# Two transformer blocks on one Trainium2 core: sliding attention one head at a time beside the rotary products, with values stationary; retention normalised head by head; probabilities scaled on GpSimd

## The reference

```python
q_a, k_a, v_a, q_r, k_r, v_r, g_r = jnp.split(rms_norm(x, g) @ w_in, splits, axis=-1)
# sliding attention: 8 heads of 64, two key/value heads, blocks of 128 queries
# see their own 128 keys (causal) and the 128 before (those within the window)
probs = softmax(concat([scores / 8, sink]))[..., :-1];  attn = probs @ v_a
# retention: 4 heads of 128, q and k turned by position, decay in place of softmax
o = (rot(q_r) @ rot(k_r).T * decay) @ v_r           # causal, all 512 tokens
o = (o - mean(o)) * rsqrt(var(o) + eps)             # for each token and head
ret = silu(g_r) * o
x = x + rms_norm(concat([attn, ret]) @ w_out, post)
```

## Time and profile before

| | |
|---|---|
| median of three runs | 2179.32 us (2174.88 to 2185.81) |
| the profiled execution | 2190.08 us, its span 2188.3 us |
| TensorE busy (PE) | 2093.4 us, 96% of the span |
| VectorE, ScalarE, GpSimd busy | 1043.9 us (48%), 822.4 us (38%), 279.7 us (13%) |
| mean granted TensorE clock | 0.973 |
| the chain that ended last, by engine | PE 80%, DVE 6%, ACT 4%, POOL 4%, issue 2% |

### The profile page before, as it was taken

The page is one execution under the profiler, slowest core; times in us unless marked ns, Lnnn a source line. Parts: engine busy times, 40 slices in busy tenths (PEclk is TensorE's granted clock), DMA queues, the critical chain, the costliest instruction groups (busy, mean ns, idle before and its releaser), DMA issues.

```text
span 2188.3 us, 25825 instructions
## 1 busy us (share of the span) xinstructions
PE 2093.4 (96%) x10292; PEld 1741.5 (80%) x10292; DVE 1043.9 (48%) x1627; ACT 822.4 (38%) x1518; POOL 279.7 (13%) x271
## 2 busy tenths in 40 slices
PE   7999999999999999999999899899999999999998
PEld 6878888888878888887887679677777888888886
DVE  5436465555335222333654666665655544222333
ACT  5225253333334222233324653355555323222232
POOL 1000100000000000000002422166664000000000
PEclk9997799999999999999999899999999999999999
DMA  5330133333322323332442034211114423333331
GB/s 193 111 92 1 49 107 96 97 96 96 97 87 97 93 92 95 97 96 77 139 141 68 1 123 142 73 58 44 44 44 147 135 75 106 96 96 97 97 96 68
DMA packets 58983, 200.14 MB, mean 91 GB/s; under 512 B 8080, under 2 KB 8112, under 8 KB 58480
## 3 DMA queue, kind: packets, MB, share of 16 engines
q1 hardware_dynamic: 53936, 178.29, 26.2%
q0 software_dynamic: 4928, 20.21, 2.6%
HBM read 181.16 MB, written 8.39 MB: 87 GB/s over the span
## 4 chain that ended last, share of the span: by engine, by line
PE 80%; DVE 6%; ACT 4%; POOL 4%; issue 2%; DVEq 1%; DMA 1%; POOLq 1%; SPq 0%; ACTq 0%
PE ps L655 25%; PE ps L654 25%; PE ps L653 25%; POOL PU L609 4%; DMA raw<-in_w_all 1%; PE ps L1067 1%; ACT Pb L1354 1%; DVE XN L1690 1%; DVE HTl L1699 1%; PE ps L983 1%; DVEq L2185 1%; DVE AUl L2190 1%; PE ps L828 1%; POOLq L598 1%; PE ps L898 1%
## 5 line engine op out<-in xcount | busy, mean ns | idle before, releaser
L1650 DVE TENSOR_TENSOR Wl<-raw,Wh 128x1024 fp32r<-128x1024 f32 x307 | 378.0, 1234 | 784.2 <-ACT Wh L1188 783.2
L653 PE MATMUL ps<-HTh,Wh 128*128 128x512 f32 (+1 forms) x1696 | 642.6, 379 | 15.9 <-DVE HTl L1699 9.7
L655 PE MATMUL ps<-HTh,Wl 128*128 128x512 f32 (+1 forms) x1696 | 647.5, 382 | 0.0
L654 PE MATMUL ps<-HTl,Wh 128*128 128x512 f32 (+1 forms) x1696 | 646.3, 381 | 0.0
L1188 ACT CAST Wh<-raw 128x1024 fp32r<-128x1024 f32 x307 | 321.2, 1050 | 841.0 <-DMA raw<-in_w_all 841.0
L653 PEld LDWEIGHTS ps<-HTh,Wh 128*128 128x128 f32 x1696 | 326.7, 193 | 81.1 <-issue 15.2
L654 PEld LDWEIGHTS ps<-HTl,Wh 128*128 128x128 f32 x1696 | 320.7, 189 | 60.9
L655 PEld LDWEIGHTS ps<-HTh,Wl 128*128 128x128 f32 x1696 | 320.5, 189 | 58.1
L653 PE MATMUL ps<-Wh,Yh 128*128 128x512 f32 x528 | 208.1, 394 | 4.3 <-DVE Yl L1826 4.3
L655 PE MATMUL ps<-Wh,Yl 128*128 128x512 f32 x528 | 206.5, 391 | 0.0
L654 PE MATMUL ps<-Wl,Yh 128*128 128x512 f32 x528 | 205.0, 388 | 0.0
(11 more groups left out here) (273 smaller groups left out, 2524.5 us busy)
## 6 DMA issues: line engine op xcount, KB each, us to landing
raw<-in_w_all SPq DMA_DIRECT2D x307, 512.0 KB, 3.5
swp_d<-qkd SPq DMA_DIRECT2D x64, 64.0 KB, 2.8
g_dram<-gst SPq DMA_DIRECT2D x16, 256.0 KB, 4.0
ring<-g_dram POOLq DMA_DIRECT2D x16, 256.0 KB, 3.6
gpre<-in_g_pre POOLq DMA_DIRECT2D x5, 512.0 KB, 5.0
X<-in_x SPq DMA_DIRECT2D x4, 512.0 KB, 5.1
swp_r<-qkr SPq DMA_DIRECT2D x16, 128.0 KB, 3.8
cw1k<-in_cw POOLq DMA_DIRECT2D x1, 2048.0 KB, 8.3
```

Of the source, the lines that this page charges most:

```text
L653: tensor.matmul(dst, a_hi, b_hi, start=start, stop=False)
L654: tensor.matmul(dst, a_hi, b_lo, start=False, stop=False)
L655: return tensor.matmul(dst, a_lo, b_hi, start=False, stop=stop)
L1650: vector.tensor_tensor(Wl[:, s, :], raw[:, s, :], Wh[:, s, :], ALU.subtract).then_inc(w_lo, 1)
```

## The change

1. **Sliding attention becomes eight units, one for each head**, in the form of the sparse stage: scores of the four query tiles in banks 0 and 1 (128 + 256 and 256 + 256 columns), four maxima with the sink, four exponentials, factors, scaling on GpSimd, seven transposes into banks 2 and 3, high and low parts, and values as stationary operand (`vhla`, high and low part side by side) into bank 4 or 5. The result is already transposed (`CATT`), so it needs no transposes later. The mask is one bf16 product of up to 256 columns (`band`).
2. **These units stand between the chunks of `rope_r`**, which uses banks 6 and 7 only. Beside the last two units stand the products of `vg`'s first four chunks for token tile 3, in the same two banks. The wait for masks and preparations comes after the first rotary chunk.
3. **Retention is normalised head by head**: statistics straight from PSUM, one square root for each head, normalising into `CAT` on VectorE, gate product on GpSimd, four transposes on TensorE into bank 6 or 7.
4. **`out1` starts with attention's four chunks**, first for token tiles 0 and 1, then, after the transposes of heads 2 and 3, for tiles 2 and 3. `cat` is gone.
5. GpSimd's loads of `cos`, `sin` and `gpost` come before the gate products, that of `gpre` after them.
6. **`cmp_vals` moves from behind the fifth to behind the seventh product of `rope_q`**, and ScalarE's share (zeros filled with values, `vcz`) with it.
7. Places in SBUF change (`slots` starts at another offset, `cst` moves). The helpers of `da` lose the case distinction; their instructions stay.

```diff
-    ("rope_r", 8, [2, 2, 2, 2, 0, 0, 0, 0], [0] * 8),
+    ("rope_r", 8, [0, 0, 0, 0, 0, 0, 4, 4], [0] * 8),
+    ("local", 0, [0] * 8, [8, 8, 8, 8, 4, 4, 0, 0]),
...
-        slots = (nc.sbuf_base + 127) // 128 * 128
+        slots = (nc.sbuf_base + 383) // 512 * 512 + 128
...
+        LOCAL = [(0, 0, 0, 0), (0, 128, 128, 1), (1, 0, 384, 2), (1, 256, 640, 3)]
...
+                def local_weigh(h):
+                    pl.wait_ge(l_gate, h + 1)
+                    for b, o, p, i in LOCAL:
+                        w = P if i == 0 else 2 * P
+                        x = PL[:, h % 2, p:p + w]
+                        last = pool.tensor_scalar(x, x, lsum[:, h % 2, i:i + 1], None, ALU.mult)
+                    last.then_inc(l_prob, 1)
...
-                pl.wait_ge(gn_rs, 1)
-                pool.tensor_tensor(ret_out, ret_out, by_tile(mv[:, :, 0]), ALU.subtract)
-                pool.drain()
-                pool.tensor_tensor(ret_out, ret_out, by_tile(grs[:]), ALU.mult)
-                pool.drain()
...
-                pool.tensor_tensor(CAT[:, :, 512:], CAT[:, :, 512:], sg[:], ALU.mult).then_inc(cat_ret, 1)
+                def gated(h):
+                    one = slice(h * P, (h + 1) * P)
+                    pl.wait_ge(free[4 + h % 2], FREED["ret"][4 + h % 2] + h // 2 + 1)
+                    pool.tensor_tensor(CAT[:, :, one], CAT[:, :, one], sg[:, :, one], ALU.mult).then_inc(cat_ret, 1)
...
+                def local_scores(h):
+                    kv = h // 4
+                    for b, o, p, i in LOCAL:
+                        if i % 2 == 0:
+                            bank_free("local", b, h)
+                        w = P if i == 0 else 2 * P
+                        k = slice(0, P) if i == 0 else slice((i - 1) * P, (i + 1) * P)
+                        q = qa[h // 4][:, h % 4, i * P:(i + 1) * P]
+                        dst = ps[b][:, o:o + w]
+                        tensor.matmul(dst, q, kah[:, kv, k], start=True, stop=False)
+                        tensor.matmul(dst, q, kal[:, kv, k], start=False, stop=False)
+                        last = tensor.matmul(dst, identb[:], band[:, 2 * P - w:], start=False, stop=True)
...
+                def local_values(h):
...
+                        tensor.matmul(dst, v, ALh[:, a], start=kb == 0, stop=False)
+                        last = tensor.matmul(dst, v, ALl[:, a], start=False, stop=kb == 3)
...
+                rope_r(0)
+                pe.wait_ge(in_c2, 16 * 9)
+                pe.wait_ge(boot, 2)
...
+                local_scores(0)
+                local_scores(1)
+                rope_r(1)
+                for h in range(8):
+                    local_turn(h)
+                    if h < 6:
+                        local_scores(h + 2)
+                        rope_r(h + 2)
+                    else:
+                        vg(2 * (h - 6), (3,), False)
+                        vg(2 * (h - 6) + 1, (3,), False)
+                    local_values(h)
             if on("vg"):
-                gemm_t("vg")
+                for c in range(4):
+                    vg(c, (0, 1, 2), True)
+                for c in range(4, 8):
+                    vg(c, range(TT), True)
...
+                ret_scores(0)
+                ret_scores(1)
                 for b in range(8):
                     pe.wait_ge(free[b], FREED[ret][b])
...
+                ret_values(0)
+                ret_scores(2)
+                ret_values(1)
+                ret_scores(3)
+                ret_turn(0)
+                ret_values(2)
+                ret_turn(1)
+                ret_values(3)
+                pe.wait_ge(ct_lo, 4)
+                for c in range(4):
+                    chunk_t("out1", c, *ht_lhs(c), c == 0, False, tiles=(0, 1), last_part=False)
+                ret_turn(2)
+                ret_turn(3)
+                for c in range(4):
+                    chunk_t("out1", c, *ht_lhs(c), c == 0, False, tiles=(2, 3))
...
-                cmp_vals()
                 rope_q(5)
                 rope_q(6)
+                cmp_vals()
                 cmp_turn(0)
...
+                rope_out(0)
+                local_exps(0)
+                rope_out(1)
+                local_exps(1)
+                for h in range(8):
+                    local_high(h)
+                    if h:
+                        local_low_rows(h - 1)
+                    if h < 6:
+                        local_exps(h + 2)
+                        rope_out(h + 2)
+                local_low_rows(7)
...
-                    if c == 5:
+                    if c == 6:
                         filled("cmp", 1, 1)
...
+                for h in range(8):
+                    local_low(h)
+                    if h < 7:
+                        local_gate(h + 1)
+                    if h:
+                        local_sum(h - 1)
+                    if h < 6:
+                        local_max(h + 2)
+                    if h < 7:
+                        rope_turned(h + 1)
+                    if h < 6:
+                        split(CHUNK0["rope_r"] + h + 2 + LEAD)
+                local_sum(7)
...
+                decayed(0)
+                decayed(1)
+                ret_stats(0)
+                decayed(2)
+                ret_norm(0)
+                ret_stats(1)
+                decayed(3)
+                ret_norm(1)
+                for k in range(4):
+                    ve.wait_ge(ht_hi, 8 * HT_STAGES.index("cat") + k + 1)
+                    vector.tensor_tensor(HTl[:, k, :], CATT[:, k, :], HTh[:, k, :], ALU.subtract).then_inc(ct_lo, 1)
+                ret_stats(2)
+                ret_low(0)
+                ret_norm(2)
+                ret_stats(3)
+                ret_low(1)
+                ret_norm(3)
+                ret_low(2)
+                ret_low(3)
```

More of the change, by code:

```diff
@@ L690, in gemm_n, with chunk_t @@
                 last.then_inc(w_used, 1)
-            def chunk_t(stage, c, lh, ll, first, final, it=0, tiles=range(TT)):
+            def chunk_t(stage, c, lh, ll, first, final, it=0, tiles=range(TT), last_part=True):
                 s = weights(CHUNK0[stage] + c, it)
@@ L854, in attend @@
[L854 to L869 removed]
+                    three(dst, Qst[:, u, m, 0, q], Qst[:, u, m, 1, q], Kst[:, u, 0, 0:w], Kst[:, u, 1, 0:w], True, False)
@@ L872, in _, with attention @@
+            def attention():
+                scores(0)
+                scores(1)
+                for t in range(TOTAL):
+                    if exists(t - 2):
+                        values(t - 2)
+                    if exists(t + 2):
+                        scores(t + 2)
+                    turn(t)
+                values(TOTAL - 2)
+                values(TOTAL - 1)
             pe.wait_ge(in_c, 16 * 2)
@@ L1945, in _, with attention @@
+            def attention():
+                maxima(0)
+                maxima(1)
+                for t in range(TOTAL):
+                    combine(t)
+                    if exists(t - 1):
+                        low(t - 1)
+                    if exists(t + 2):
+                        maxima(t + 2)
+                low(TOTAL - 1)
             vector.memset(eps[:], EPS)
@@ L2027, in _, with ret_stats @@
-            if on("cat"):
-                to_ht("cat", HTh, HTl)
+                def ret_stats(h):
+                    filled("ret", 4 + h % 2, h // 2)
+                    for i in range(4):
+                        vector.bn_stats(bn[:, 4 * h + i, :], ps[4 + h % 2][:, i * P:(i + 1) * P])
+                    vector.drain()
+                    for i in range(4):
+                        last = vector.bn_aggr(mv[:, 4 * h + i, :], bn[:, 4 * h + i, :])
+                    vector.drain().then_inc(gn_mv, 1)
@@ L2046, in _ @@
             if on("da"):
-                attention("da")
+                attention()
             if on("nsf"):
```

549 lines of the change are left out of this document (252 added, 297 removed).

## The result

After the change the kernel takes 2114.28 us, median of four runs (2113.61 to 2119.6), against 2180.49 (2174.88 to 2185.81) before: ratio 0.9702, 95% interval 0.9673 to 0.9731. The forecast was 2127 with a range from 2112 to 2150, so the time lies in the range, near its lower end. The profiled executions have spans of 2188.3 and 2112.4 us, 75.9 apart; the sum said 51.9. (The medians are 66.2 apart: the execution of the kernel before that was profiled, 2190.08 us, is slower than all four timed ones, and that of the kernel after, 2114.19, lies at its median.) Some 26 us thus came from something that the sum doesn't contain, and one of its own terms turned out too favourable. The experiments are about both.

A forecast was written before the change was run, and what follows sets the result against it. TensorE was taken as the bound nearly everywhere, in the mixing stage at half speed by short products. Terms -73.1 + 31.4 - 1.9 - 8.3 = -51.9, from the median 2179.3, gave 2127 us, range 2112 to 2150.

The forecast's parts named there:

- the sum: Whole kernel: stretches on TensorE add up to 51.9 us saved.
- B: Rotary products, attention units and v/gate: from 92.3 to 123.7 us, 31.4 more; bounds 115 and 137.
- A step: Steps 0 to 5, one unit and one rotary chunk each: 3.3 + 5.55 = 8.85 us on TensorE.
- scores(1): Second unit's scores wait for maxima and exponentials of scores(0), whose banks they use: TensorE idles 2.1 us.
- the last unit: Step 6, with only 2.8 us of v/gate beside the unit: 2.2 us of idle, bounds 0.6 and 4.
- rival 1: VectorE becomes the bound of a step beside GpSimd's work: steps 10.3 to 10.5, 11 us more, 2138; chance 0.15.
- The 1.2 us for ScalarE's order: Scores(2) wait 1.2 us for exponentials(1), which ScalarE takes up only after evicting rotary chunk 1.
- C: Into retention: TensorE's idle of 2.9 us becomes 1.0, 1.9 saved.
- D: Compressed values: two ready rotary products go first, idle and half-clock loss vanish, 8.3 us saved (bounds 0 and 8.3).
- A: Retention to the fourth chunk of the output product: from 115.9 to 42.8 us, 73.1 saved.
- the bound of 49: Upper bound for A: a 6.0 us spell at half clock costs 3.0, GpSimd at twice its price 2 x 1.3.
- Rivals 2 and 5: Clock stays lower through B, 2198, chance 0.05; each head waits for its own chain, 28 more, 2155, chance 0.07.

The follow-up runs named there:

- e2_after_slots256: Changed kernel with the weight slots back at 256 modulo 512 (95488 bytes instead of 95360): 2143.65 us, ratio 0.9811 to the kernel before.
- e4_after_early_halves: Changed kernel with the high and low parts of attention's result made during v/gate products instead of in retention: 2107.09 us, ratio 0.9653 to the kernel before.
- e7_after_serial: Changed kernel with the eight attention units behind the eight rotary chunks instead of between them, on all engines: 2147.47 us, ratio 0.9827 to the kernel before.

## Why the prediction was right, and where it was not

**What bounded the kernel: right.** TensorE was the bound, at half speed through sliding attention. That is gone: the turns of the units have no idle and the granted clock is 1.00 from 90 to 130 us.

**B, forecast 123.7, measured 121.9: right, for slightly other sums.** A step was to be 8.85 us and is 8.55. At a distance of 0.680 us for a group, its 24 rotary products take 5.44 (forecast 5.55), which leaves 3.1 for a unit (forecast 3.3). With the slots at the place of before the whole stretch is about 123.3 us (`e2_after_slots256`, retention from 186.28 with 0.92 of idle before it), 0.4 from the forecast. The idles came where they were looked for: 2.15 us before scores(1) (forecast 2.1) and 2.13 at the last unit (2.2). The clock cost 21.8 x 0.08 + 15 x 0.11 = 3.4 (3.0). The 1.2 us for ScalarE's order didn't appear; a wait of 0.68 for GpSimd at the first turn did, and 0.5 us of the idle at the last unit has the same cause (rival 1 below).

**C and D: right.** 1.2 us of idle for 1.0; no idle at the compressed values, and for 8.3 us 8.7 in the trace, 5.7 (1.5 to 10.1) in the median when done alone.

**A, forecast 42.8, measured 47.0: a step that failed.** The prediction gave each gate product 1.3 us, took the four subtractions of `HTl` as ready at 17.9, and asked of them only whether VectorE was in time. It did not lay GpSimd's second gate product, at the same moment, beside them. That product took 3.44 us, TensorE waited 3.8 instead of 0.7, and the clock fell to 0.61 for the next 4.4 us. The stretch lies within the bound of 49, which had a spell at half clock in it. `e4_after_early_halves` shows that it was this pair: without it the stretch takes 43.2, which is 0.4 from the forecast.

**Rival 1, VectorE as the bound of a step: the right pair, but the other engine gave way.** VectorE beside GpSimd's scaling is not slowed: groups by line and shape, 90 to 130 us of the kernel after.

```profile
L485 POOL TENSOR_SCALAR PL<-PL,lsum 128x256 f32<-128x256 f32 x15 | 17.9, 1210 | 0.0
L1710 DVE TENSOR_TENSOR Wl<-raw,Wh 128x1024 fp32r<-128x1024 f32 x5 | 6.1, 1225 | 5.4 <-ACT Wh L1218 5.4
...
L1996 DVE TENSOR_TENSOR qkr<-qkr,cos 128x512 f32<-128x512 f32 x5 | 3.4, 686 | 0.0
```

The rotary operations take 0.69 us and the split 1.23, the mean of before. GpSimd's 1.210 is a mean of two kinds (and so is the twin's 1.076 of the earlier trace rows: six of its seven took 0.92). The second and third scaling of a unit, beside VectorE's sum and maxima with at most one input in SBUF, take 0.93 us. The last one starts inside VectorE's rotary operations, which have two. GpSimd's timeline from 112.5 us and VectorE's beside it:

```profile
112.42 1.75 POOL L485 TENSOR_SCALAR PL<-PL,lsum 128x256 f32<-128x256 f32 x1
```

```profile
112.17 0.68 DVE L1810 TENSOR_TENSOR swp_r<-swp_r,sin 128x512 f32<-128x512 f32 x1
112.78 0.69 DVE L1996 TENSOR_TENSOR qkr<-qkr,cos 128x512 f32<-128x512 f32 x1
113.54 0.73 DVE L1998 TENSOR_TENSOR qkr<-qkr,swp_r 128x512 f32<-128x512 f32 x1
```

It ends 0.7 us behind the second of them and has lost 0.82. `e7_after_serial` has no rotary operation beside the units, and there all 24 scalings of this shape take their 0.92 us:

```profile
L485 POOL TENSOR_SCALAR PL<-PL,lsum 128x256 f32<-128x256 f32 x24 | 21.8, 924 | 0.0
```

So one input in SBUF is enough for GpSimd to be kept waiting by VectorE's operations with two. In most steps this is hidden: the four scalings took 4.13 us, above the 3.8 allowed for, where 3.31 would do without the wait. At the two ends it shows. Beside the first unit's scalings stood three rotary operations and a split. The first two took 1.46 and 2.23 us, 2.2 more than usual, and by these numbers TensorE's 0.68 at the first turn would not be there without that. At the last unit one scaling lost 0.5 us. In `e4_after_early_halves` the DMA of the swap landed 1.0 us later there, VectorE began the rotary operations later, the scalings took 3.31 and TensorE's idle was 1.64 instead of 2.13.

In the other direction the loss is smaller. By the Trainium skill (page SBUF — State Buffer, section "SBUF: two separate sides") it is whichever starts first that keeps the other out, so VectorE should wait for a scaling that is under way. The operation at 112.17 started inside the scaling from 111.53 to 112.45 and took 0.68 us all the same. There the trace does not agree. One that started 0.05 us behind a scaling, at 138.19 in `e4_after_early_halves`, took 0.97, 0.3 more than usual and less than the scaling's length:

```profile
138.19 0.97 DVE L1812 TENSOR_TENSOR swp_r<-swp_r,sin 128x512 f32<-128x512 f32 x1 [1.81 <-DMA swp_r<-qkr]
```

In the earlier trace rows the loss was 0.84 us: GpSimd's subtraction, with two inputs in SBUF, had begun 0.3 us before VectorE's split, in the kernel before:

```profile
1369.22 1.29 POOL L601 TENSOR_TENSOR QSn<-qnr,QSn 64x512 fp32r<-64x512 f32 x1
```

The prediction carried this price, of a GpSimd operation with two inputs, over to scalings with one, and put it on the wrong engine.

**Rivals 2 and 5: not here.** The clock held in the mixture; and that the units do lie beside the rotary chunks is worth 27 to 33 us (`e7_after_serial`).

**Item 7, places in SBUF: never priced.** It gave 24 to 29 us, about two fifths of the whole saving. Without it the kernel gets to 2143.65, 16.6 above the forecast, still in the range. No row of the trace before shows what another place would do, so its bounds were open on both sides, and that had to be said: an edit that moves an operand of 2304 groups costs 23 us for each 10 ns of a group's distance. Some two fifths of the gain were hidden in a line that the sum passed over.

**From the profiled execution to the median: too favourable, and luck.** The sum was read in an execution of the kernel before that lay 10.8 us above the median and then taken from the median. Without item 7 the profiled spans differ by 50.3, close to the 51.9, but the times by 41 (34 to 49). Executions of the kernel before lie between 2172 us, at a mean clock of 0.983, and 2194, at 0.972, so what is saved depends on which one is read. Which stretches hold the 10.8 us stays open. The forecast of 2127 lies as near to 2114 as it does because two errors had opposite signs: 24 to 29 us that the sum left out, and some 11 that it counted too much.

## What to carry to other kernels

Read a line that moves a buffer as an edit to every product that reads it: count products in a stretch that is wholly busy at clock 1.00, before and after, and the placement shows at once. When a step of one engine goes to another, lay the two engines' operations out in time against each other, not only against their deadlines: four VectorE subtractions with two SBUF inputs, begun just ahead of GpSimd's product of two, kept it waiting for their whole length, and a scaling with one input waited behind two. And long products beside a chain of short, dependent ones are worth both the idle and the clock, if each step's chain stays under its TensorE time.

## What the hardware showed that was not expected

- Three 512-column products with weights stationary take 0.680 us from start to start with the slots of the weights' low halves at 128 or 384 bytes past a multiple of 512, and 0.693 at 0 or 256. It is 1.2% of this kernel. With weights moving the start of the other tiles counts too: 0.687 before, 0.697 with the slots alone moved, 0.680 with both.
- GpSimd's 512-column product of two SBUF operands took 3.44 us instead of 1.27 when four VectorE subtractions with two SBUF inputs had started 0.17 us before it, and those were not slowed. Its 256-column scaling, with one SBUF operand, took 1.75 us instead of 0.93 when a VectorE operation with two had started 0.25 us before it.
- The granted clock fell behind TensorE's idles of 2.13, 2.15 and 3.81 us in the kernel after, and stayed at 1.00 behind 1.64 us in `e4_after_early_halves`. The same wait at unit 7 was one in the first kernel and the other in the second, and with it came or went some 1.6 us of clock. The length of one idle does not decide alone: in `e7_after_serial`, with an idle in every step, the clock kept 1.00 behind 1.62 us (142.6 to 149.0) and was 0.67 on the mean between 157.2 and 162.0, behind 1.64.
